# First norm of a two-layer backbone kernel: who computes the modulation, and in which order

## The chip, the cores and the metric

The kernel runs on one core of one Trainium2 chip. The metric is the device time of one execution in microseconds. Engines are called PE (TensorE), DVE (VectorE), ACT (ScalarE), POOL (GpSimd) and SP (the queue that issues most loads).

## The reference, cut to what matters

Two layers over 512 latent and 256 context tokens of width 1024. All modulation comes from two conditioning vectors (one for latents, one for context) through a SiLU and a large matrix, 9 x 1024 outputs a layer:

```python
sc = jax.nn.silu(c); scc = jax.nn.silu(c_ctx)
m  = (sc  @ w_mod[i] + b_mod[i]).reshape(Bsz, 1, N_MOD, D_MODEL)
mc = (scc @ w_mod[i] + b_mod[i]).reshape(1, 1, N_MOD, D_MODEL)
x  = _half_ffn(x,  norm_g[i, 0], m,  0, w1, w3, w2)   # then a mixer, then a second half FFN
xc = _half_ffn(xc, norm_g[i, 0], mc, 0, w1, w3, w2)
```

A half FFN norms its input (RMS over the width), multiplies by one plus a scale and adds a shift, both from the modulation, computes `silu(h @ w1) * (h @ w3) @ w2`, and adds half of that times a gate, also from the modulation. Nothing of the first half FFN can start before the first norm, and the norm's output needs scale (1024 values, eight tiles of 128) and shift (eight more) for both vectors. The gate (eight tiles) is needed only by the down-projection.

## The kernel before, in words

Activations lie transposed: `x` is 128 partitions x 8 chunks x 768 tokens. Each f32 product is made of three fp32r products, of a high and a low part of both operands: ACT writes the high part (`split_hi`, L1362, and `weight_hi`), DVE the low one (`split_lo`, L2014, and `weight_lo`), PE multiplies hi by hi, hi by lo and lo by hi (`gemm_step`, L698 to L702). Weights come in tiles of 128 x 1024 (512 KB) through two buffers `raw`, loaded by SP in a fixed order.

**The first norm.** The first 24 tiles of the modulation matrix are loaded whole: tiles 0 to 7 are the shift, 8 to 15 the scale, 16 to 23 the gate (`gmini`). A tile is either multiplied on PE (`PE_MINI`, L1325: eight f32 matmuls of two columns, the two vectors in `sc`; each shows in the trace as two instructions) or, in another layout, on DVE (`DVE_MINI`): one `dot` (L2019) per vector, a product of 128 x 1024 with the broadcast vector, with a sum along the row into `M`. Before the change seven tiles are PE's and nine DVE's, in order of number. ACT squares the eight chunks of `x`, POOL adds seven of them (`add_squares`, L2899), PE sums over the partitions with a matrix of ones (`norm_sums`, L751 and L754, its place is ahead of tile 11), ACT makes `rstd` by Ln and Exp (L1504, L1505). DVE does its eighteen dots, two weight splits among them, adds the bias, makes the scale `modA` (`prep`), and then runs `norm`: `scaled(j)` writes x times scale times rstd (L2292), ACT adds the shift (L1516, `xh`), `rest(j)` writes the low part (L2284, `xl`) and releases chunk j to PE. Four chunks are scaled before the first `rest`. PE then multiplies the first two weight tiles together (`gemm_pair`), chunk by chunk as they are released.

**The first FFN** (f = 0) has 22 hidden chunks in groups of 4, 6, 6, 6. A group multiplies its up tiles (two per hidden chunk), and then its eight down tiles (j = 0 to 7) into `x`. Group 0 is plain (`plain_pair`). Groups 1 to 3 use seven half-size products per chunk (`seven_products`, weights A11, S1, S2, S34, A12, A22), whose sums of weight blocks POOL prepares in DRAM by accumulating DMAs (`weight_sums`), starting right after its `add_squares`. Between all this DVE computes the remaining modulation. `gate_dots(i)`, i = 0 to 3, four dots each, stood ahead of and behind the hidden chunks 0 and 1. The later "mods" (120 tiles, two dots each) are placed by a table, `mod_places`: so many at an up chunk or down tile; their loads go through two buffers `mraw`, issued on ACT's queue two mods ahead (`next_mods`), each after the dots of the mod before last in the same buffer. `take_scb` applies the SiLU to the broadcast vectors (`scb`) that all those dots use; before the change that was ahead of the FFN.

Engines take their instructions in program order; waits are on semaphores.

Of the kernel before, what the change touches and what calls it, by code (L numbers as in the profile page):

```python
# [22 lines left out]
P = 128  # L23
# [128 lines left out]
def mod_places():  # L152
    where = []
    for f in range(3):
# [8 lines left out]
        if f == 0:  # L163
            place["down", 1, 2] = place["down", 2, 2] = 2
# [43 lines left out]
def build(nc, dr):  # L208
    ctx = ExitStack()
    with ctx:  # L210
# [70 lines left out]
        mini = [at(f"mini{j}", [P, D], XH + j * D) for j in range(2 * KC)]  # L281
        gmini = [at("gmini0", [P, 4, D], H + 4 * D), at("gmini1", [P, 4, D], H)]
# [129 lines left out]
        def sem(name):  # L412
# [3 lines left out]
        par_landed, con_landed, x_landed, out_stored = sem("par_landed"), sem("con_landed"), sem("x_landed"), sem("out_stored")  # L416
# [14 lines left out]
        sc_ready, eps_set, prep_done = sem("sc_ready"), sem("eps_set"), sem("prep_done")  # L431
# [19 lines left out]
        wdt_landed, wdt_hi, wdt_lo, dt_mm, dt_copied, dt_abs, dt_act, dt_set, dve_chain = (  # L451
            sem(n) for n in ("wdt_landed", "wdt_hi", "wdt_lo", "dt_mm", "dt_copied", "dt_abs", "dt_act", "dt_set", "dve_chain"))
# [49 lines left out]
        def heads(col, n, width):  # L502

            return col.unsqueeze(2).to_broadcast([P, n, width])

# [58 lines left out]
        def _(sp):  # L564
# [73 lines left out]
            for j in range(2 * KC):  # L638
                src = dr["wmk"][PE_MINI.index(j)] if j in PE_MINI else dr["wmn"][j]
                sp.dma_start(mini[j][:], src).then_inc(mini_landed[group(j)], 16)  # L640
                if j == KC:
                    sp.dma_start(con[:], dr["con"]).then_inc(con_landed, 16)
                if j in (10, 12):
                    s = j // 2 - 5
# [703 lines left out]
        def _(act):  # L1348
# [625 lines left out]
            for j in range(KC):  # L1974
                square(j, 0, x[:, j, :], T)
# [1133 lines left out]
```

## Time and profile before

| | us |
|---|---|
| median of 3 runs | 2787.57 (2786.97 to 2790.0) |
| the profiled execution, its own time | 2784.83 |
| span of the profile | 2783.1 |
| PE busy | 2675.1 (96%) |
| DVE busy | 2056.2 (74%) |
| ACT busy | 1176.3 (42%) |
| POOL busy | 390.2 (14%) |

Times in rows are microseconds from the start of the span. A row of the timeline gives the start, the length, engine, line, operation, output and inputs, the count merged into it, and in brackets how long the engine was idle before it and what ended that. A start with "q" behind the engine's name is that engine's queue issuing a DMA.

### The profile page before, as it was taken

How to read it: one execution, taken by the hardware profiler on the slowest of the kernel's cores; microseconds unless marked ns; L12 is line 12 of the kernel's file. 1: busy time of each engine (PE TensorE's matmuls, PEld its weight loads, DVE VectorE, ACT ScalarE, POOL GpSimd, SP SyncE). 2: the span in 40 equal slices, each digit the busy share in tenths (PEclk: the TensorE clock that was granted, in tenths of full speed). 3: DMA queues.
4: the chain of work that ended last, by engine and by line, in shares of the span. 5: the costliest groups of instructions: out<-in, count | busy, mean ns of one | idle time of the engine just before them, and what ended most of it. 6: DMA issues, size and time to landing. Idle time of an engine off the chain costs nothing.

```text
span 2783.1 us, 40131 instructions
## 1 busy us (share of the span) xinstructions
PE 2675.1 (96%) x15624; PEld 2512.6 (90%) x15624; DVE 2056.2 (74%) x3184; ACT 1176.3 (42%) x1860; POOL 390.2 (14%) x312
## 2 busy tenths in 40 slices
PE   5999999999988999999999999999999989999999
PEld 5999999998976899999999999999997775788898
DVE  7887878774558587878777877787878667666674
ACT  3233333346447644332323523242436866533342
POOL 3111111110012521111111211100022410211000
PEclk8999999999999999999999999999999999999999
DMA  9888989621120047889897589874522110378453
GB/s 347 209 228 248 274 252 267 169 67 54 59 62 1 1 143 203 245 224 281 229 274 212 137 221 258 248 214 131 165 69 83 61 46 1 114 201 235 145 165 125
DMA packets 161691, 464.13 MB, mean 167 GB/s; under 512 B 13281, under 2 KB 14433, under 8 KB 160609
## 3 DMA queue, kind: packets, MB, share of 16 engines
q1 hardware_dynamic: 87200, 247.65, 26.3%
q0 software_dynamic: 56448, 146.81, 24.3%
q10 hardware_dynamic: 17856, 67.12, 6.8%
q8 instruction: 125, 2.05, 0.3%
q14 instruction: 62, 0.50, 0.0%
HBM read 459.43 MB, written 148.90 MB: 219 GB/s over the span
## 4 chain that ended last, share of the span: by engine, by line
PE 78%; DVE 11%; DMA 5%; ACT 3%; issue 3%; POOL 0%; ACTq 0%; SPq 0%; DVEq 0%; POOLq 0%
PE banks L698 11%; PE banks L702 11%; PE banks L700 11%; PE banks L786 9%; PE banks L788 9%; PE banks L787 9%; DMA raw<-sums 4%; PE banks L705 3%; PE banks L709 3%; PE banks L707 3%; DVE banks L2019 1%; DVE tmp L2292 1%; PE banks L1233 1%; DVE wl L2086 1%; DVE wl L2014 1%
## 5 line engine op out<-in xcount | busy, mean ns | idle before, releaser
L1362 ACT ACTIVATE wh<-raw 128x1024 fp32r<-128x1024 f32 (+2 forms) x194 | 181.8, 937 | 611.8 <-PE banks L702 458.7
L2019 DVE SCALAR_TENSOR_TENSOR banks<-mraw,scb 128x1024 f32<-128x1024 f32 x240 | 304.9, 1270 | 11.6 <-DMA mraw<-in_wmn 7.9
L2014 DVE TENSOR_TENSOR wl<-raw,wh 128x1024 fp32r<-128x1024 f32 (+2 forms) x216 | 234.3, 1085 | 95.5 <-ACT wh L1362 93.2
L1427 ACT ACTIVATE wh<-raw 128x512 fp32r<-128x512 f32 (+1 forms) x210 | 161.6, 774 | 326.6 <-DMA raw<-sums 156.7
L698 PE MATMUL banks<-hh,wh 128*128 128x384 f32 x1056 | 270.4, 337 | 9.3 <-DVE wl L2014 9.0
L786 PE MATMUL banks<-xh,wh 128*128 128x384 f32 (+1 forms) x796 | 258.0, 324 | 12.8 <-DVE wl L2086 12.7
L702 PE MATMUL banks<-hh,wl 128*128 128x384 f32 x1056 | 269.9, 336 | 0.0
L700 PE MATMUL banks<-hl,wh 128*128 128x384 f32 x1056 | 269.7, 336 | 0.0
L788 PE MATMUL banks<-xh,wl 128*128 128x384 f32 (+1 forms) x796 | 256.6, 322 | 0.0
L787 PE MATMUL banks<-xl,wh 128*128 128x384 f32 (+1 forms) x796 | 256.5, 322 | 0.0
L698 PE MATMUL banks<-xh,wh 128*128 128x384 f32 x880 | 230.7, 343 | 21.4 <-DVE xl L2284 12.0
L700 PE MATMUL banks<-xl,wh 128*128 128x384 f32 x880 | 225.2, 336 | 0.0
L702 PE MATMUL banks<-xh,wl 128*128 128x384 f32 x880 | 224.9, 336 | 0.0
L2086 DVE TENSOR_TENSOR wl<-raw,wh 128x512 fp32r<-128x512 f32 (+1 forms) x210 | 180.9, 866 | 43.6 <-ACT wh L1427 43.5
L698 PEld LDWEIGHTS banks<-hh,wh 128*128 128x128 f32 x1056 | 191.5, 189 | 11.5 <-DVE wl L2014 11.2
L702 PEld LDWEIGHTS banks<-hh,wl 128*128 128x128 f32 x1056 | 192.3, 189 | 0.0
L700 PEld LDWEIGHTS banks<-hl,wh 128*128 128x128 f32 x1056 | 192.2, 189 | 0.0
L698 PEld LDWEIGHTS banks<-xh,wh 128*128 128x128 f32 x880 | 158.4, 189 | 29.9 <-issue 16.0
L786 PE MATMUL banks<-th,wh 128*128 128x384 f32 (+1 forms) x560 | 180.5, 322 | 0.0
L787 PE MATMUL banks<-tl,wh 128*128 128x384 f32 (+1 forms) x560 | 180.5, 322 | 0.0
L788 PE MATMUL banks<-th,wl 128*128 128x384 f32 (+1 forms) x560 | 180.5, 322 | 0.0
L786 PEld LDWEIGHTS banks<-xh,wh 128*128 128x128 f32 x796 | 150.0, 188 | 16.3 <-DVE wl L2086 16.3
(427 smaller groups left out, 6225.5 us busy)
## 6 DMA issues: line engine op xcount, KB each, us to landing
raw<-sums SPq DMA_DIRECT2D x140, 512.0 KB, 6.0
sums<-in_w POOLq DMA_DIRECT2D x88, 768.0 KB, 8.5
mraw<-in_wmn ACTq DMA_DIRECT2D x120, 512.0 KB, 5.7
a<-in_w SPq DMA_DIRECT2D x70, 512.0 KB, 4.3
sums<-in_w POOLq DMA_DIRECT2D x22, 1536.0 KB, 8.8
sums<-sums POOLq DMA_DIRECT2D x44, 768.0 KB, 9.6
raw<-in_w SPq DMA_DIRECT2D x80, 384.0 KB, 4.3
raw<-in_w SPq DMA_DIRECT2D x52, 512.0 KB, 3.9
```

The source lines that it names most:

```text
L698: pe.matmul(bank(h), W, tokens(rh, h), start=(k == 0), stop=False)
L700: pe.matmul(bank(h), W, tokens(rl, h), start=False, stop=False)
L702: mm = pe.matmul(bank(h), L, tokens(rh, h), start=False, stop=(k == nk - 1))
L705: pe.matmul(G[slot][:, a:b], W, rh[:, k, a:b], start=(k == 0), stop=False)
L786: pe.matmul(thirds(bank), W, rh(k), start=(k == 0), stop=False)
L787: pe.matmul(thirds(bank), W, rl(k), start=False, stop=False)
L788: mm = pe.matmul(thirds(bank), L, rh(k), start=False, stop=(k == 3))
L1362: act.activation(wh[slot][:, 0:nk * P], raw[slot][:, 0:nk * P], ACT.Copy).then_inc(hi_done, 1)
L1427: act.activation(W_HI[slot_of(name, last)], W_SRC[name], ACT.Copy).then_inc(w_hi, 1)
L2014: dve.tensor_tensor(wl[slot][:, 0:nk * P], raw[slot][:, 0:nk * P], wh[slot][:, 0:nk * P].bitcast(F32), ALU.subtract).then_inc(lo_done, 1)
L2019: return dve.scalar_tensor_tensor(B67[:], tile, 1.0, scv[:, s, :], ALU.mult, ALU.mult, accum_out=out)
L2086: dve.tensor_tensor(W_LO[to], W_SRC[name], W_HI[to].bitcast(F32), ALU.subtract).then_inc(w_lo, 1)
```

## The change

It deals the sixteen first tiles anew: PE gets 8 to 12, 0 to 2 and 4 to 6 in this order, DVE 13, 14, 15, 3 and, behind the scaling of the first chunks, 7. The loads follow that order, in eight groups; `x` is loaded in halves, the first weight tiles come ahead of them. Tiles 0 to 7 now lie where the gate tiles go later, so these are loaded after the shifts have been used. PE multiplies parameters by parameters into the norm's bank, a result nobody reads, eight times ahead of tile 8 and four times ahead of tiles 10 and 0 (512 columns, f32). The norm's sums move ahead of tile 0 and are one product, as DVE now adds all eight squares, which ACT writes to eight places of their own. Tiles 4 to 6 wait until ACT has made `rstd`, whose bank they use. The shift is added in two halves inside `norm`. The gate dots use `scb0` and stand one place later each; `take_scb` follows hidden chunk 1. Hidden chunk 2 has no mods of its own any more; down tile 5 of groups 1 and 2 has two instead of one.

```diff
-PE_MINI = (1, 3, 5, 7, 9, 11, 13)
-DVE_MINI = (0, 2, 4, 6, 8, 10, 12, 14, 15)
-MINI_GROUPS = ((0, 1, 2), (3, 4, 5, 6), (7, 8, 9, 10), (11, 12, 13), (14, 15))
+PE_MINI = (8, 9, 10, 11, 12, 0, 1, 2, 4, 5, 6)
+DVE_MINI = (13, 14, 15, 3, 7)
+MINI_GROUPS = ((8, 9, 13), (10, 11, 14), (12, 15), (0, 3), (1, 2), (4, 7), (5,), (6,))
+WARM = {8: 8, 10: 4, 0: 4}
...
         if f == 0:
-            place["down", 1, 2] = place["down", 2, 2] = 2
+            place["up", 2] = 0
+            place["down", 1, 2] = place["down", 2, 2] = place["down", 1, 5] = place["down", 2, 5] = 2
...
+                        if (f, g, i) == (0, 0, 1):
+                            load_gate_minis()
...
+            def load_gate_minis():
+                for q in range(2):
+                    sp.wait_ge(mini_mm, 2 + q)
+                    sp.wait_ge(mini_dot, (9, 12)[q])
+                    sp.dma_start(gmini[q][:], dr["wmn"][16 + 4 * q:20 + 4 * q].rearrange("t p n -> p t n")).then_inc(gmini_landed, 16)
+                sp.dma_start(wdt[:], dr["wdt"]).then_inc(gmini_landed, 16)
+
             sp.dma_start(par[:], dr["par"]).then_inc(par_landed, 16)
+            for s in range(2):
+                sp.dma_start(raw[s][:, 0:D], dr["w13"][s]).then_inc(raw_landed[s], 16)
             sp.dma_start(scb0[:], dr["ccb"]).then_inc(scb_landed, 16)
-            sp.dma_start(x[:], dr["x"]).then_inc(x_landed, 16)
...
+            for q, js in enumerate(MINI_GROUPS):
+                for j in js:
+                    src = dr["wmk"][PE_MINI.index(j)] if j in PE_MINI else dr["wmn"][j]
+                    sp.dma_start(mini[j][:], src).then_inc(mini_landed[q], 16)
+                if q < 2:
+                    half_k = slice(4 * q, 4 * q + 4)
+                    sp.dma_start(x[:, half_k, :], dr["x"][:, half_k, :]).then_inc(x_landed[q], 16)
+                if q == 0:
+                    sp.dma_start(con[:], dr["con"]).then_inc(x_landed[0], 16)
...
+                if n == 0:
+                    for a, b, _s in segs:
+                        mm = pe.matmul(NP[:, a:b], cst("ones"), ssq[:, a:b], start=True, stop=True)
+                    mm.then_inc(norm_sum, 1)
+                    return
...
             for j in PE_MINI:
-                if j == 11:
-                    pe.wait_ge(con_landed, 16)
+                for _ in range(WARM.get(j, 0)):
+                    pe.matmul(NP[:, 0:512], par[:, 0:P], par[:, 0:512], start=True, stop=True)
+                if j == 0:
+                    pe.wait_ge(x_landed[0], 32)
                     norm_sums(0, SEGS)
-
+                if j == 4:
+                    pe.wait_ge(rstd_ready, 1)
...
                 for j in range(KC):
+                    if n == 0 and j % 4 == 0:
+                        act.wait_ge(mini_dot, (9, 12)[j // 4])
...
-                        if 0 < f < 3 and ch == 1:
-                            take_scb(f + 2, scb)
+                        if f < 3 and ch == 1:
+                            take_scb(f + 2 if f else 1, scb)
...
+            act.wait_ge(par_landed, 16)
+            act.activation(sc[:].rearrange("p k s -> p (k s)"), pr("cc"), ACT.Silu).then_inc(sc_ready, 1)
+            split_hi(0, 0, 0, KC)
+            split_hi(1, 1, 0, KC)
             act.wait_ge(scb_landed, 16)
             act.activation(scb0[:], scb0[:], ACT.Silu).then_inc(scb_ready, 1)
...
             for j in range(KC):
-                square(j, 0, x[:, j, :], T)
...
+                if j % 4 == 0:
+                    act.wait_ge(x_landed[j // 4], (32, 16)[j // 4])
+                act.activation(squares[j][:], x[:, j, :], ACT.Square).then_inc(sq_done, 1)
             norm(0, SEGS, lambda j: None)
             load_scb(scb)
-            take_scb(1, scb)
...
                         def ahead():
+                            if f == 0 and 1 <= ch < 3:
+                                gate_dots(2 * ch - 1)
+                            if f < 3:
+                                dot_mods(f, ("up", ch))
+
+                        def behind():
                             if f == 0 and ch < 2:
                                 gate_dots(2 * ch)
...
+            def shift_batch(q):
+                dve.wait_ge(mini_mm, 2 + q)
+                dve.wait_ge(mini_dot, (8, 11)[q])
+                first_bias(4 * q, 3, 4).then_inc(mini_dot, 1)
+                dve.wait_ge(mini_dot, (9, 12)[q])
+
+            def first_between(q):
+                if q == 0:
+                    shift_batch(0)
+                    first_dots(7, 9)
+                if q == 1:
+                    shift_batch(1)
+
+            chain(dve.memset(eps[:], EPS))
+            split_lo(0, 0, KC)
+            split_lo(1, 1, KC)
+            dve.wait_ge(scb_ready, 1)
+            first_dots(13, 0)
+            for j in range(1, 4):
+                add_square(j)
+            first_dots(14, 2)
+            for j in range(4, KC):
+                add_square(j)
+            first_dots(15, 4)
+            first_dots(3, 6)
             dve.wait_ge(par_landed, 16)
             dve.wait_ge(mini_mm, 1)
...
             prep(0)
-            norm(0, SEGS, lambda s: None)
+            norm(0, SEGS, first_between)
...
-            add_squares(0, T)
+            pool.wait_ge(mini_landed[len(MINI_GROUPS) - 1], 16 * len(MINI_GROUPS[-1]))
             for g in (1, 2, 3):
                 weight_sums(0, g)
```

`first_dots(j, n)` is two dots of tile j, `add_square(j)` one add of 128 x 768 into `ssq`, `first_bias` two small adds.

## Rows read from the trace of the kernel before

**Rows 1.** The page: busy us, share of the span, instructions
```profile
PE 2675.1 (96%) x15624; PEld 2512.6 (90%) x15624; DVE 2056.2 (74%) x3184; ACT 1176.3 (42%) x1860; POOL 390.2 (14%) x312
```

**Rows 2.** Timeline of PE, 17 to 60 us
```profile
22.41 13.81 PE L1325 MATMUL banks<-sc,mini 128*128 128x2 f32 x64 [1.36 <-DMA mini<-in_wmn]
36.09 2.91 PE L751 MATMUL banks<-ssq,con 128*128 128x512 f32 x4
...
41.35 3.79 PE L1325 MATMUL banks<-sc,mini 128*128 128x2 f32 x32
57.09 0.98 PE L698 MATMUL banks<-xh,wh 128*128 128x384 f32 x2 [11.96 <-DVE xl L2284]
```

**Rows 3.** Windows: busy per engine; then PE's granted clock, DMA share, GB/s
```profile
45.00:46.00 1.00, 0.13 (x2) 0.04 (x1) 0.97 (x3) 0.98 (x2) 0.46 (x1) 0.54 0.48 193
...
61.00:62.00 1.00, 1.00 (x4) 1.00 (x4) 1.00 (x3) 0.78 (x2) 0.00 (x0) 0.50 1.06 264
62.00:63.00 1.00, 1.00 (x7) 1.00 (x7) 1.00 (x3) 0.34 (x1) 0.00 (x0) 0.93 1.12 284
```

**Rows 4.** Timeline of DVE up to the first norm's chunks
```profile
18.81 2.65 DVE L2019 SCALAR_TENSOR_TENSOR banks<-mini,scb 128x1024 f32<-128x1024 f32 x1
...
49.32 1.23 DVE L2019 SCALAR_TENSOR_TENSOR banks<-mini,scb 128x1024 f32<-128x1024 f32 x1
...
51.57 4.32 DVE L2292 SCALAR_TENSOR_TENSOR tmp<-x,modA,rstd 128x512 f32<-128x512 f32 x8
...
55.80 2.21 DVE L2284 SCALAR_TENSOR_TENSOR xl<-tmp,M,xh 128x512 fp32r<-128x512 f32 x4
```

**Rows 5.** Timeline of ACT: landings of x and weights, rstd
```profile
13.71 1.58 ACT L1479 ACTIVATE sq<-x 128x768 f32<-128x768 f32 x2 [5.45 <-DMA x<-in_x]
...
33.40 1.06 ACT L1362 ACTIVATE wh<-raw 128x1024 fp32r<-128x1024 f32 x1 [2.68 <-DMA raw<-in_w]
...
41.64 1.28 ACT L1504 ACT_TABLE_LOAD   x1 [7.19 <-PE banks L754]
...
45.15 0.84 ACT L1505 ACTIVATE rstd<-sq 128x768 f32<-128x768 f32 x1
```

**Rows 6.** Timeline around the end of the first pair of products
```profile
67.66 1.28 ACT L1375 ACT_TABLE_LOAD   x1
...
76.33 0.79 ACT L1391 ACTIVATE tmp<-banks 128x768 f32<-128x768 f32 x1
...
77.73 0.61 PE L698 MATMUL banks<-xh,wh 128*128 128x384 f32 x2 [1.42 <-DVE wl L2014]
```

**Rows 7.** Timeline of DVE at the end of group 0's up tiles
```profile
127.98 0.95 DVE L2049 TENSOR_TENSOR tmp<-tmp,banks 128x768 f32<-128x768 f32 x1
```

**Rows 8.** Timeline of ACT's DMA queue, down tiles of groups 1 and 2
```profile
293.67 0.33 ACTq L1368 DMA_DIRECT2D mraw<-in_wmn  x1
...
432.01 0.33 ACTq L1368 DMA_DIRECT2D mraw<-in_wmn  x1
```

**Rows 9.** Timeline of DVE at the turn to the next group
```profile
304.36 0.88 DVE L2203 SCALAR_TENSOR_TENSOR x<-banks,modG,x 128x256 f32<-128x256 f32 x2 [0.64 <-PE banks L702]
...
312.85 0.69 DVE L2086 TENSOR_TENSOR wl<-a,wh 128x512 fp32r<-128x512 f32 x1
...
444.41 0.88 DVE L2203 SCALAR_TENSOR_TENSOR x<-banks,modG,x 128x256 f32<-128x256 f32 x2 [0.64 <-PE banks L702]
```

**Rows 10.** Timeline of PE: the A12 product of group 2's first chunk
```profile
314.60 0.33 PE L786 MATMUL banks<-xh,wh 128*128 128x384 f32 x1
```

**Rows 11.** Landing of mod tiles: whole run (page, last number), 285 to 310, 425 to 450
```profile
mraw<-in_wmn ACTq DMA_DIRECT2D x120, 512.0 KB, 5.7
...
DMA to landing us min/median/max: 4.1/6.1/8.2
...
DMA to landing us min/median/max: 5.0/7.0/9.0
```

**Rows 12.** Timeline of POOL at the second norm
```profile
540.58 1.40 POOL L2896 COPY ssq<-sq 128x768 f32<-128x768 f32 x1 [15.87 <-ACT sq L1479]
```

More of the change, by code:

```diff
@@ L277, in pr @@
             return par[:, PCOL[n][0]:PCOL[n][1]]
-        mini = [at(f"mini{j}", [P, D], XH + j * D) for j in range(2 * KC)]
-        gmini = [at("gmini0", [P, 4, D], H + 4 * D), at("gmini1", [P, 4, D], H)]
+        mini = [at(f"mini{j}", [P, D], (H if j < KC else XH - KC * D) + j * D) for j in range(2 * KC)]
+        gmini = [at(f"gmini{q}", [P, 4, D], H + 4 * q * D) for q in range(2)]
+        squares = [ssq, sq[0], sq[1], tmp[0], tmp[1], tmp[2], tmp[3], rstd]
         scb0 = at("scb0", [P, 2, D], HID + 2 * HC * T - 3 * T)
@@ L504, in heads, with mini_out @@
             return col.unsqueeze(2).to_broadcast([P, n, width])
+        def mini_out(j, n=1):
+            bank = G[0][:, 0:512] if j >= KC else G[0][:, 512:1024] if j < 4 else NP
+            return bank[:, 2 * j:2 * (j + n)]
         def group(j):
@@ L1615, in ab_in_act @@
                     if c == 3:
-                        act.wait_ge(wdt_landed, 16)
-                        act.activation(wdh[:], wdt[:], ACT.Copy).then_inc(wdt_hi, 1)
+                        act.wait_ge(gmini_landed, 48)
+                        act.activation(wdh[:], wdt[:], ACT.Copy).then_inc(dt_act, 1)
                         act.activation(ea[:, 0, :], pr("alog"), ACT.Exp).then_inc(dt_act, 1)
@@ L2268, in gate_dots @@
                         dve.wait_ge(mini_dot, n0 + 2 * q + s)
-                        dot(gmini[q // 4][:, q % 4, :], s, scb, M[:, 16 + q, s:s + 1]).then_inc(mini_dot, 1)
+                        dot(gmini[q // 4][:, q % 4, :], s, scb0, M[:, 16 + q, s:s + 1]).then_inc(mini_dot, 1)
                 dve.wait_ge(mini_dot, n0 + 4 * i + 4)
@@ L2857, in _, with add_square, first_bias @@
                     dot(mini[j][:], s, scb0, M[:, j, s:s + 1]).then_inc(mini_dot, 1)
-                if q in (6, 7):
-                    split_lo(q - 6, q - 6, KC)
+            def add_square(j):
+                dve.wait_ge(sq_done, j + 1)
+                if j > 1:
+                    dve.wait_ge(ssq_acc, j - 1)
+                dve.tensor_tensor(ssq[:], ssq[:], squares[j][:], ALU.add).then_inc(ssq_acc, 1)
+            def first_bias(j, n_pe, n):
+                bias = pr("bmod")[:, j:j + n].unsqueeze(2).to_broadcast([P, n, 2])
+                dve.tensor_tensor(M[:, j:j + n_pe, :], mini_out(j, n_pe).rearrange("p (t s) -> p t s", s=2), bias[:, 0:n_pe], ALU.add)
+                return dve.tensor_tensor(M[:, j + n_pe:j + n, :], M[:, j + n_pe:j + n, :], bias[:, n_pe:n], ALU.add)
@@ L2864, in _ @@
-            for js, src in ((slice(1, 14, 2), pairs), (slice(0, 15, 2), M), (slice(15, 16), M)):
-                n_ = len(range(16)[js])
-                chain(dve.tensor_tensor(M[:, js, :], src[:, js, :], pr("bmod")[:, js].unsqueeze(2).to_broadcast([P, n_, 2]),
-                                        ALU.add))
+            dve.wait_ge(mini_dot, 8)
+            chain(first_bias(KC, 5, KC))
             prep(0)
-            norm(0, SEGS, lambda s: None)
+            norm(0, SEGS, first_between)
```

62 lines of the change are left out of this document (18 added, 44 removed).

## The prediction

> **What bounds the kernel now.** I read the page first. PE is busy for 96% of the span [rows 1], so what the change touches, the first 57 us, is nearly the only long stretch without useful matmuls, and what it can give is small beside 2783 us.
>
> Then the timeline, engine by engine. PE works through seven narrow tiles (two columns each), squeezes the norm's sums in between, and then stands idle for 11.96 us until the first real matmul at 57.09, released by DVE's `xl` [rows 2]. DVE has eighteen dots to do, a dot is 2.65 us while POOL adds squares and 1.30 us after that, the last starts at 49.32, and only then, at 51.57, can it scale the first chunk, though `rstd` was there at 45.99 [rows 4, 5]. So DVE's dots set the start: 57.09 = 51.57, plus 4.23 for four scaled chunks, plus 1.1 for `rest(0)`.
>
> The clock needs care. The granted clock is 1.00 in the windows before 45 and half in 45.1 to 62.1 [rows 3], but durations tell of more: 64 narrow instructions take 13.81 us from 22.41, 32 take 3.79 us from 41.35 [rows 2]. One tile is 16 of them: 3.45 us before 41.4, 1.90 us after. I read this as 1.2 GHz up to about 41.5, 2.4 GHz up to 45.1, 1.2 GHz again until 62.1. It rose some 5.2 us after wide matmuls began (36.09 to 41.5, 57.09 to 62.1) and fell 3.6 us after they ended (41.4 to 45.1), although narrow tiles filled those 3.6 us. I use these two delays below.
>
> **Landings.** `x` lands at 13.71, the second weight tile at 33.40 [rows 5]; between them 13 tiles, the constants and two weight tiles land, 8072 KB in 19.69 us, 410 KB/us. The new order on the same queue gives: first group 12.5, half of `x` with constants 17.2, second group 20.9, other half 24.7, then 27.1, 29.6, 32.1, 34.6, 35.9, 37.1.
>
> **A. The start of the first up-projection.** DVE loses 8 of 18 dots ahead of the norm's scaling (five tiles are ten dots, two of them tile 7's, moved behind it) and gains seven adds; a 128x768 add is about 0.95 us. POOL no longer runs beside it, so a dot is 1.30. In order: tile 13 to 15.1, three adds behind ACT's squares to 21.7, tile 14 to 24.3, four adds to 29.2, tiles 15 and 3 to 34.4, bias and prep to about 35. It isn't late any more.
>
> PE is. `sc` is ready near 3.9. A 512-column f32 matmul is 5.26 us x 512/1536 = 1.75 us at 1.2 GHz [rows 2], so 0.88 at 2.4. Eight fillers: 5.2 us slow (3 of them), five fast, to 13.5. Tiles 8 and 9 at 1.90: 17.3; there the clock falls. Four fillers, 5.2 + 0.9: 23.4. Tiles 10 and 11: 27.2. Tile 12, slow: 30.7. Four fillers: 36.8. The two sums of 768 columns, now fast: 38.1. ACT then needs what it took from 41.56 to 45.99 [rows 5]: `rstd` at 42.5.
>
> Two paths lead from there to the first real matmul.
> - DVE: 4.25 (four scaled) + 0.5 (bias of the first shifts) + 2.65 (tile 7's two dots, which now stand ahead of `rest(0)`) + 1.2 = 51.1.
> - PE: tiles 0 to 2, 3.6 us fast and the rest slow, to 45.5; tiles 4 to 6, slow, 3 x 3.45 = 10.35, to 55.9. They must be through before the first matmul, as PE works in order.
>
> PE ends last: 55.9 for 57.09, a gain of 1.2 us. DVE's supply and ACT's, delayed by waits on the shifts, still run ahead of it, and the second shift bias waits only for tile 6. The pair of products that follows starts at half clock as before and keeps its 19.2 us. Bounds from the rows: if the third fillers and tiles 0 to 2 all run fast, 51.5 (gain 5.6); if the third fillers and the sums are slow and tiles 0 to 2 too, 60.9 + 0.1 (loss 3.9). I take the walk's value, whose delays are the measured ones.
>
> **B. The Silu table.** Today ACT loads Silu's table at 67.66, for `take_scb`, while it waits for nothing else, and the first Silu of `G[0]` starts at 76.33, straight behind the split of the third tile [rows 6]. With `take_scb` one chunk later, the table load of 1.28 us falls between that split and this Silu, which frees the bank that the third product needs. It would end at 77.12 + 1.28 = 78.4 on today's scale against 77.67, when `wl` was there [rows 6]: +0.8. Bounds 0 (the load is hoisted) and 1.3.
>
> **C. Costed at nothing.** Gate dots: ch 0 loses four, ch 2 exchanges four mod dots for four gate dots. PE has no wait from 77.73 to the end of this group, and the last multiply, at 127.98 [rows 7], follows PE's product by 0.2 us, so at most 0.2 comes back. If that cover went, four dots would be 5.3 us. On SP, `load_gate_minis` stands after tiles 2 and 3 and waits for the second shift batch, near 57; behind it only loads wait that need the split of tile 2 at 76. The gate tiles (4 MB, 10 us) then land by 70, needed near 80. On POOL, `weight_sums` starts at 37 for 31, but its first block is then free of the initial loads; at the next norm POOL had waited 15.87 us for ACT [rows 12], more than these 6 us and the earlier start together. Were that gone, ACT's squares would wait. DVE's split of the first weights comes earlier, in idle time.
>
> **D. The two mods that move to the sixth down tile of groups 1 and 2.** Each is 2.65 us more of DVE in one tile, and one more load in a chain of two buffers. In group 1 the second mod's load is the one issued at 293.67 [rows 8]. With the page's 5.7 us to landing [rows 11] it lands at 299.4. Then: two dots to 302.0, `x` of j=6 to 303.2, three splits of 0.6 to 305.0, the two dots of j=6 to 307.7. `x` of j=7 started at 304.36 [rows 9]: DVE is 3.3 us late. ACT, which issues loads behind dots, issues the next one at 308.1, it lands 0.45 after DVE wants it. From that `x` on DVE runs without a gap to the split for A12, which ends at 313.45 and is wanted by PE at 314.60 [rows 9, 10], slack 1.15. Stall: 3.3 + 0.45 - 1.15 = 2.6. In group 2 the load is that of 432.01, landing 437.7, dots to 440.4, and by the same steps `x` at 446.0 for 444.41: 1.6 + 0.45 - 1.15 = 0.9 (slack taken as equal). Together +3.5. Bounds by landings seen just there [rows 11]: at 4.1 and 5.0 us the stalls are 0.95 and 0.1, sum 1.0; at the stretches' medians of 6.1 and 7.0 some 3.4 and 3.6, sum 7.0; at the maxima near 11. I take the page's median, as only few of the neighbours' issues are these. PE being in order, what is lost isn't given back.
>
> **Sum:** -1.2 + 0.8 + 0 + 3.5 = +3.1 us; less 0.2 at most from C: +2.9. Against the profiled execution, 2784.8, that is 2787.7. The median of the runs, 2787.6, lies 2.7 above the profiled one, so I give 2790.5.
>
> **Rivals.** A difference under 0.2% (5.6 us) can't be told from no change here.
> 1. *The moved dots are hidden* (D = 0: landings as short as 4 us, or slack that I don't see). -1.2 + 0.8 - 0.2 = -0.6: 2787.0. For it: f=0 had two such tiles without a PE wait. Against: those lie four tiles ahead of the turn to the next group, these two.
> 2. *The clock stays up through the narrow tiles*, as they follow wide ones without a gap. Walk: fillers to 13.5, tiles 17.3, fillers 20.8, tiles 24.7, tile 12 29.0, fillers 32.5, sums 33.8, `rstd` 38.2, tiles 0 to 2 39.5, 4 to 6 45.2, DVE's path 46.9. The first real matmul at 47, and the pair all fast: its 19.2 us hold 5.0 at half clock, so 16.7. It ends at 63.7 for 76.3, -12.6. Sum -12.6 + 0.8 - 0.2 + 3.5 = -8.5: 2779.1. Against: the fall at 45.1, with narrow tiles running to 45.14 [rows 2, 3]. The Trainium skill (TensorE: Matmul & The Clock Gate, Why this matters for your kernels) asks for no idle gaps between bursts to keep the full clock; by that rule narrow tiles back to back would hold it and the sum would be this rival's, but this trace does not agree, by the fall just named.
> 3. *DVE falls further behind* (the other side): landings as in the stretches, D = 7.0: +6.4, 2794.0. It decides once a mod takes more than about 6.5 us to land at both turns; for it speak the medians of 6.1 and 7.0 [rows 11].
> 4. *The fillers don't raise the clock*, the change doesn't do what it says: all at 1.2 GHz PE ends tile 12 at 42.1, the sums at 51.7, tile 6 at 72.4: +15.3 + 4.1 = +19.4, 2807. Against: two rises behind wide matmuls.
>
> **Chances.** Likeliest 0.52 (its own range 2787 to 2794), rival 1 0.20, rival 2 0.10, rival 3 0.15, rival 4 0.03. Faster by over 0.2%: rival 2 and a tail, 0.12. Slower: rival 4, most of rival 3, a tail of the likeliest, 0.22. Within: 0.66. The range 2783 to 2797 leaves out rivals 2 and 4 and tails.
>
> **What would show it.** In the profile after: the first matmul of the pair at 55.9, released by PE's own narrow tiles, not by `xl`; narrow tiles 4 to 6 at 0.21 us an instruction; `rstd` near 42.5, dots of 1.23 us throughout; an ACT table load right ahead of the first Silu of `G[0]`; new PE waits on `wl` at the first A12 of groups 2 and 3 of the first FFN. The prediction is wrong if PE is on 2.4 GHz in tiles 4 to 6, if the sums come much before 38, if the waits at the turns are missing or above 8 us, or if POOL's sums come late.

## The result and the profile after

The changed kernel is slower by a quarter of a per cent: 2794.56 us in the median of 18 runs (2785.86 to 2803.76), the kernel before 2789.84 in 18 runs beside them (2775.01 to 2797.72), ratio 1.0027 with a 95% interval of 1.0015 to 1.0039. The ratio is worth 7.5 us, the medians differ by 4.7. Single executions of one kernel lie up to 23 us apart (the two ends for the kernel before), so each profile below is one draw from such a spread: the profiled execution of the changed kernel took 2803.39 us, at the upper end of its own runs.

I read the start first. Timeline of PE in the kernel after, up to the first real matmul, to be held against [rows 2]:

```profile
3.92 8.52 PE L1339 MATMUL banks<-par 128*128 128x512 f32 x16 [3.92 <-ACT sc L1994]
13.24 3.73 PE L1347 MATMUL banks<-sc,mini 128*128 128x2 f32 x32 [0.81 <-DMA mini<-in_wmn]
16.84 5.38 PE L1339 MATMUL banks<-par 128*128 128x512 f32 x8
22.05 3.63 PE L1347 MATMUL banks<-sc,mini 128*128 128x2 f32 x32
29.63 3.58 PE L1347 MATMUL banks<-sc,mini 128*128 128x2 f32 x16 [3.95 <-DMA mini<-in_wmn]
33.07 5.86 PE L1339 MATMUL banks<-par 128*128 128x512 f32 x8
38.76 1.45 PE L766 MATMUL banks<-ssq,con 128*128 128x512 f32 x4
40.05 16.61 PE L1347 MATMUL banks<-sc,mini 128*128 128x2 f32 x96
56.52 0.99 PE L712 MATMUL banks<-xh,wh 128*128 128x384 f32 x2
```

The idle 11.96 us of [rows 2] are gone and PE's own narrow tiles stand right ahead of the first real matmul. It comes at 56.52, only 0.57 us sooner. DVE was ready well before, as its timeline shows: it waits for `rstd` and scales from 43.42 on, where it began at 51.57 [rows 4]. PE's row shows the other half: tiles 0 to 2 and 4 to 6, 96 instructions, run until the first real matmul.

```profile
43.42 4.32 DVE L2314 SCALAR_TENSOR_TENSOR tmp<-x,modA,rstd 128x512 f32<-128x512 f32 x8 [7.00 <-ACT rstd L1527]
```

Then the end of the first pair of products, which answers to [rows 6]: ACT's timeline, PE's first matmul of the third product, and windows of one microsecond behind it (busy time by engine, then PE's granted clock, DMA share, GB/s).

```profile
74.69 1.06 ACT L1384 ACTIVATE wh<-raw 128x1024 fp32r<-128x1024 f32 x1 [10.84 <-PE banks L716]
75.77 1.28 ACT L1413 ACT_TABLE_LOAD   x1
77.06 0.81 ACT L1413 ACTIVATE tmp<-banks 128x768 f32<-128x768 f32 x1
```

```profile
78.02 0.63 PE L712 MATMUL banks<-xh,wh 128*128 128x384 f32 x2 [2.38 <-ACT tmp L1413]
```

```profile
78.00:79.00 1.00, 0.98 (x4) 1.00 (x5) 1.00 (x2) 0.86 (x2) 0.00 (x0) 0.71 1.17 215
79.00:80.00 1.00, 1.00 (x4) 1.00 (x4) 1.00 (x2) 0.81 (x1) 0.00 (x0) 0.50 1.07 274
80.00:81.00 1.00, 1.00 (x4) 1.00 (x4) 1.00 (x3) 0.00 (x0) 0.25 (x1) 0.50 1.11 397
81.00:82.00 1.00, 1.00 (x5) 1.00 (x5) 1.00 (x1) 0.00 (x0) 0.98 (x1) 0.58 0.92 299
```

The table load stands between the split and the first Silu of `G[0]`, and PE waits 2.38 us where it waited 1.42. The wait brought more than itself: behind it the clock falls to half for some 3.4 us, which costs another 1.7 us of work (1 minus the clock, summed over the four windows). Behind the wait of 1.42 in the kernel before it didn't fall.

Now the turns to the next group. The profile's waits of PE, 300 to 350 and then 430 to 480 us (total, times, longest):

```profile
PE banks L805 <- DVE wl L2109: 2.3, 1, 2.3
PE banks L805 <- DVE wal L2109: 1.5, 1, 1.5
...
PE banks L805 <- DVE wl L2109: 6.6, 2, 5.6
```

The kernel before has 0.9 us of such waits in the first stretch and none in the second. DVE's timeline at both turns, against [rows 9] (the reads of the accumulator behind each dot are left out):

```profile
302.27 1.23 DVE L2042 SCALAR_TENSOR_TENSOR banks<-mraw,scb 128x1024 f32<-128x1024 f32 x1 [1.47 <-DMA mraw<-in_wmn]
...
310.20 0.87 DVE L2226 SCALAR_TENSOR_TENSOR x<-banks,modG,x 128x256 f32<-128x256 f32 x2
...
319.27 0.68 DVE L2109 TENSOR_TENSOR wl<-a,wh 128x512 fp32r<-128x512 f32 x1
...
453.55 0.87 DVE L2226 SCALAR_TENSOR_TENSOR x<-banks,modG,x 128x256 f32<-128x256 f32 x2
...
458.31 1.23 DVE L2042 SCALAR_TENSOR_TENSOR banks<-mraw,scb 128x1024 f32<-128x1024 f32 x1
...
463.06 1.23 DVE L2042 SCALAR_TENSOR_TENSOR banks<-mraw,scb 128x1024 f32<-128x1024 f32 x1 [3.46 <-DMA mraw<-in_wmn]
...
465.88 0.68 DVE L2109 TENSOR_TENSOR wl<-a,wh 128x512 fp32r<-128x512 f32 x1
```

And why the dot at 463.06 had to wait: ACT and its DMA queue at the second turn.

```profile
447.53 1.15 ACT L1449 ACTIVATE wh<-raw 128x512 fp32r<-128x512 f32 x2 [8.72 <-DVE banks L2042]
...
454.16 1.06 ACT L1449 ACTIVATE wh<-raw 128x1024 fp32r<-128x1024 f32 x1 [5.47 <-DVE banks L2042]
...
459.63 0.34 ACTq L1390 DMA_DIRECT2D mraw<-in_wmn  x1
460.07 0.63 ACT L1449 ACTIVATE wh<-a 128x512 fp32r<-128x512 f32 x1 [2.92 <-DVE banks L2042]
```

The issue at 459.63 stands right behind the dot that ends at 459.5, which frees the buffer; its mod reaches DVE 3.4 us later, and the three splits that the A12 product needs stand behind that dot in DVE's order. The splits of ACT wait for DVE too (8.72, 5.47 and 2.92 us "<-DVE banks"), since ACT issues each load only when the dots before it are done, and its weight splits stand behind that. In the kernel before, ACT waited 4.87, 5.09 and 0.92 us ahead of the same splits, and PE ended those waits. So a late DVE makes the loads late, and ACT's part of the splits. What came back to DVE by the mod was 3.46 us; by ACT's splits it was 0.44 us at either turn (DVE's idle time ahead of the `wl` split at 311.90 and 455.25). PE stands still for 5.59 us and then runs at half clock, as the windows show:

```profile
466.62 0.69 PE L805 MATMUL banks<-xh,wh 128*128 128x384 f32 x1 [5.59 <-DVE wl L2109]
```

```profile
320.00:330.00 10.00, 9.99 (x48) 9.99 (x49) 8.29 (x12) 4.33 (x7) 1.22 (x1) 0.83 0.88 262
...
466.00:470.00 4.00, 3.38 (x11) 3.38 (x12) 3.74 (x6) 0.52 (x1) 0.00 (x0) 0.50 1.08 215
470.00:475.00 5.00, 5.00 (x28) 5.00 (x27) 3.14 (x5) 2.93 (x5) 0.77 (x1) 0.90 0.88 290
```

**Where the time went.** I compared the start of the same ScalarE instruction in two timelines: its lag behind the kernel before. Each figure below is the median of the lags within 12 us of that time, one profiled execution of each kernel (the experiments are told in the next section).

| us in the kernel before | 100 | 165 | 270 | 400 | 560 | 1120 | 2770 |
|---|---|---|---|---|---|---|---|
| after | +1.8 | +1.1 | +0.5 | +5.0 | +14.4 | +14.4 | +18.6 |
| after_old_mods | +0.9 | +3.6 | +3.3 | +1.0 | +2.1 | +2.2 | +8.4 |
| after_early_silu | -1.6 | -1.6 | -0.9 | +0.9 | +8.0 | +8.8 | +6.3 |
| after_both_undone | -1.5 | +1.2 | +0.9 | +1.3 | +2.6 | +3.7 | +4.0 |
| before_new_mods | +3.8 | +3.6 | +3.7 | +10.4 | +14.0 | +13.6 | +12.5 |
| before_dots_only | +0.5 | -0.4 | +0.5 | +0.4 | +1.4 | -0.8 | -5.8 |
| dots_only_again | +3.7 | +3.4 | +3.1 | +6.8 | +10.9 | +10.2 | +15.1 |
| before_one_mod_moved | +3.1 | +2.3 | +3.7 | +8.1 | +9.3 | +9.0 | +10.1 |
| mods_at_down0 | -1.7 | -1.7 | -1.8 | -2.9 | +5.3 | +3.1 | +0.7 |
| three_more_on_dve | -1.3 | +1.5 | +1.1 | +0.9 | +0.9 | +0.6 | +6.3 |
| no_fillers | -1.2 | +1.6 | +1.2 | +0.4 | +0.3 | -0.8 | +2.2 |
| gate_dots_behind | -1.5 | -1.4 | -1.9 | -4.4 | -3.4 | -3.7 | -8.2 |
| start_and_table | -7.0 | -7.0 | -5.8 | -6.5 | -4.1 | -3.1 | +2.4 |

The first line is the answer for the one execution: next to nothing until 270, 4.5 us at the first turn, 9.4 at the second, the rest late in the run, where the change touches nothing and where the other lines swing by 5 to 6 us either way.

A caution on the first columns. Four of these kernels (the two of before_dots_only, before_new_mods and before_one_mod_moved) have the code of the kernel before up to 100 us, and yet three of them are 3.1 to 3.8 us behind it there. PE's wait ahead of the third product, 1.42 us in the profile of the kernel before, is 2.53 to 3.39 us in all four. The Silu of `scb`, which stands ahead of ACT's split of that tile, waits longer for its transfer. In the kernel before it starts at 71.80, after a wait of 2.86 us; in before_new_mods, for one:

```profile
74.87 1.91 ACT L1376 ACTIVATE scb<-scb 128x2048 f32<-128x2048 f32 x1 [5.93 <-DMA scb<-in_ccb]
79.04 1.01 PE L699 MATMUL banks<-xh,wh 128*128 128x384 f32 x2 [3.39 <-DVE wl L2015]
```

So the profile of the kernel before is a lucky one at this place, and a lag of up to 4 us between two single profiles need not come from an edit. For the turns, read how a line grows from 270 to 560: +13.9 for the change, +10.3 for before_new_mods, +7.8 for dots_only_again, +5.6 for before_one_mod_moved, and -1.5 to +1.7 in the six kernels whose mods are at their old places with no dots added.

### The profile page after: what moved, and what is told of

Its sections match the earlier page's. It is cut to its first block, busy times and chain, and to the rows that moved or that the text cites. A ratio compares the mean times of both kernels' runs of the same rounds, so it can differ in the third digit from the quotient of the medians.

```text
span 2801.6 us, 40306 instructions
## 1 busy us (share of the span) xinstructions
PE 2708.0 (97%) x15716; PEld 2534.7 (90%) x15716; DVE 2044.1 (73%) x3178; ACT 1175.5 (42%) x1860; POOL 374.2 (13%) x305
## 4 chain that ended last, share of the span: by engine, by line
PE 80%; DVE 10%; DMA 4%; ACT 3%; issue 2%; POOL 0%; SPq 0%; ACTq 0%; DVEq 0%; POOLq 0%
PE banks L805 11%; PE banks L807 11%; PE banks L806 11%; PE banks L712 10%; PE banks L714 10%; PE banks L716 10%; PE banks L719 3%; PE banks L723 3%; PE banks L721 3%; DMA mraw<-in_wmn 2%; DMA raw<-sums 1%; PE banks L1252 1%; DVE tmp L2314 1%; PE banks L1091 1%; DVE wl L2037 1%
## 5 line engine op out<-in xcount | busy, mean ns | idle before, releaser
L712 PEld LDWEIGHTS banks<-hh,wh 128*128 128x128 f32 x1056 | 191.4, 189 | 12.5 <-DVE wl L2037 12.2
```

The costliest lines, as they stand in the source:

```text
L712: pe.matmul(bank(h), W, tokens(rh, h), start=(k == 0), stop=False)
```

## The experiments

Medians stand beside those of the kernel before on the same chip: 2787.91 (34 runs) for the first four; 2786.06 (34) for before_dots_only, mods_at_down0, three_more_on_dve and no_fillers; 2786.19 (31) for dots_only_again, before_one_mod_moved, gate_dots_behind and start_and_table.

**after_old_mods.** The changed kernel with all mods at their old places:

```diff
-            place["up", 2] = 0
-            place["down", 1, 2] = place["down", 2, 2] = place["down", 1, 5] = place["down", 2, 5] = 2
+            place["down", 1, 2] = place["down", 2, 2] = 2
```

> The changed kernel with the mods back in their old places (two at hidden chunk 2, one at down tile 5 of groups 1 and 2). Theory M (the two moved mods cost most of the loss, through DVE's lateness at the turns to groups 2 and 3): no PE wait on weights above 1 us at either turn, and a time of the kernel before, -4 to +3 us; hidden chunk 2 then has eight dots, which may cost up to 3 us on PE in group 0. Theory S (the loss lies ahead of the first FFN's group 1, in the late Silu table load and the clock that falls behind it): turns clean too, but the time stays 4 us or more above before.

2786.90 us, ratio 0.9998 (0.9983 to 1.0012): the loss is gone, and with it the waits at both turns. PE still waits 2.38 us for the table load.

**after_early_silu.** The moved mods kept, `take_scb(1, scb)` back ahead of `ffn(0)`:

```diff
-                        if f < 3 and ch == 1:
-                            take_scb(f + 2 if f else 1, scb)
+                        if 0 < f < 3 and ch == 1:
+                            take_scb(f + 2, scb)
...
             load_scb(scb)
+            take_scb(1, scb)
             ffn(0, KC, 1, T, T)
```

> The changed kernel with take_scb back ahead of the first FFN, nothing else. Theory S: PE's wait for the third weight tile is 1.4 us instead of 2.4, the granted clock stays 1.00 behind it, together 2.5 us less than the changed kernel, and with it most of the loss gone. Theory M: 1 to 2.5 us less than the changed kernel, which leaves 4 us or more above before, and PE still waits 3 to 7 us in sum at each of the turns to groups 2 and 3.

2793.88 us, ratio 1.0021 (1.0004 to 1.0037). In the profile the wait is 1.42 again, without the fall of the clock, and the lag at 100 us is 3.4 us better, 1.0 of it because the first real matmul came at 55.48 for 56.52. In the median that can't be told from nothing. PE still waits 3.5 and 4.0 us on weight splits at the two turns.

**after_both_undone.** Both of these diffs together; what stays is the first norm and the gate dots.

> The changed kernel with both undone: old places of the mods and early take_scb. Both theories: only the new start is left, whose first real matmul stood 0.6 us earlier than before, so -3 to +2 us against before. If it is slower by 4 us or more, something else in the start costs, such as the later weight sums on POOL.

2786.00 us, ratio 0.9990 (0.9974 to 1.0006). It differs from after_early_silu by the mods alone, and is 7.9 us faster by the medians. The lag is -1.5 us at 100 and +1.2 at 165. Between the two stands a wait that neither the kernel before nor the change has (waits of PE, 120 to 145 us):

```profile
PE banks L711 <- DVE hl L2078: 3.4, 1, 3.4
```

Eight dots, four for the gate and four for mods, stand there ahead of the product of up chunk 2. The wait stands in after_old_mods, no_fillers and three_more_on_dve too, at 3.40 or 3.41 us: every kernel with the gate dots of the change and the mods left in chunk 2. This is followed up in gate_dots_behind.

**before_new_mods.** The kernel before with the new places alone (the first diff, the other way).

> The kernel before with the new places of the mods alone: none at hidden chunk 2, two at down tile 5 of groups 1 and 2. Theory M: PE waits of 2 to 7 us in sum at each of the two turns that the kernel before does not have, and 5 to 13 us slower than before. Rival (the stalls at the turns come only together with the new start, by its later weight sums and other phase of the loads): within 2 us of before, and clean turns.

2799.21 us, ratio 1.0041 (1.0022 to 1.0060). The places alone cost as much as the whole change or more. PE at the turns:

```profile
317.14 0.66 PE L787 MATMUL banks<-th,wh 128*128 128x384 f32 x1 [2.84 <-DVE wl L2087]
325.81 0.44 PE L787 MATMUL banks<-xh,wh 128*128 128x384 f32 x1 [2.91 <-DVE wl L2087]
468.53 0.45 PE L787 MATMUL banks<-xh,wh 128*128 128x384 f32 x1 [3.29 <-DVE wl L2087]
```

So the cause was placed. Open was what of a moved mod costs: its load in the chain of two buffers, or its 2.65 us of DVE.

**before_dots_only.** The kernel before; at down tile 5 of groups 1 and 2 the two dots of the mod already there are done twice, with no load more:

```diff
                 for m in MODS[f][2].get(key, ()):
+                    if f == 0 and key in (("down", 1, 5), ("down", 2, 5)):
+                        dve.wait_ge(mod_landed[m % 2], 16 * (m // 2) + 16)
+                        dve.wait_ge(mod_dot, 2 * m)
+                        for q in range(2):
+                            chain(dot(mraw[m % 2][:], q, scb, M[:, 24 + m, q:q + 1]))
                     dot_mod(m, scb, 1 if f == 0 else f + 2, mraw)
```

> The kernel before, its mods in their old places, with two more dots on the tile already there at down tile 5 of groups 1 and 2 (same values written twice): the 2.65 us of DVE that the moved mods bring, without their load. Theory L (the load is what costs: the second mod waits for a tile that is issued behind the dots of the one before, and lands 5 to 8 us later): waits of PE at the turns 0 to 1.5 us each, 0 to +4 us against before. Rival W (DVE's plain work costs): most of the +11 us that the new places alone cost, at least +7.

2795.21 us, ratio 1.0040 (1.0024 to 1.0055). My theory that an added load was the cost fell: dots without one cost about as much. (The added dots also hold the buffer longer, so the next load is issued later; this run doesn't part that delay from DVE's own time.) But the profiled execution, 2779.08 us, was the fastest of twelve, and showed almost none of it (+1.4 at 560). A profile that disagrees with its own median explains nothing, so I ran the same kernel again.

**dots_only_again.** No edit.

> The kernel before with the two extra pairs of dots at down tile 5 of groups 1 and 2, as in before_dots_only, to see a second profiled execution: there the profile showed a lag of only 1.4 us at 600 us while the median was 9 us above the kernel before. Theory W (VectorE has no room for 2.65 us more at these turns, and how much of it shows depends on how late the transfers are in the one execution): the median again 6 to 11 us above the kernel before, and this profile shows new PE waits on wl of 2 to 8 us in all at 300 to 350 and 430 to 480 us. Rival: the median of the first measurement was a chance of it; then 0 to 3 us above, and no waits at the turns.

2793.99 us, ratio 1.0015 (0.9995 to 1.0035), profiled at 2799.96. Together the two measurements lie 8 to 9 us up by medians, 4 to 11 by ratios, and the interval of the second reaches just below 1. This profile shows what the other didn't:

```profile
321.77 0.44 PE L786 MATMUL banks<-xh,wh 128*128 128x384 f32 x1 [2.95 <-DVE wl L2091]
464.84 0.44 PE L786 MATMUL banks<-xh,wh 128*128 128x384 f32 x1 [2.29 <-DVE wl L2091]
```

Its DVE had two waits just ahead of the four dots that the fast execution had not, one for ACT's split and one for the mod; the split had itself waited 7.91 us for its weight tile:

```profile
297.51 0.85 ACT L1362 ACTIVATE wh<-raw 128x768 fp32r<-128x768 f32 x1 [7.91 <-DMA raw<-in_w]
...
298.39 0.96 DVE L2014 TENSOR_TENSOR wl<-raw,wh 128x768 fp32r<-128x768 f32 x1 [0.91 <-ACT wh L1362]
300.04 1.23 DVE L2019 SCALAR_TENSOR_TENSOR banks<-mraw,scb 128x1024 f32<-128x1024 f32 x1 [0.69 <-DMA mraw<-in_wmn]
```

In the fast one the same split and dot of DVE started at 293.53 and 294.48, with no wait ahead of either. My reading is that the extra work eats the slack in which DVE had absorbed transfers a microsecond or two late. Two profiles of this kernel fit it; they don't prove it.

**before_one_mod_moved.** The kernel before with one mod moved, from up chunk 2 to down tile 5 of group 1:

```diff
-            place["down", 1, 2] = place["down", 2, 2] = 2
+            place["up", 2] = 1
+            place["down", 1, 2] = place["down", 2, 2] = place["down", 1, 5] = 2
```

> The kernel before with one mod only moved, from up place 2 to down tile 5 of group 1; the second stays. Theory M with costs that add: the wait at the turn of group 1 (300 to 350 us) is the 3 to 6 us of the runs with both, the turn of group 2 clean, and the median 4 to 7 us above the kernel before. Rival: the two moves amplify each other (one alone hides in slack, the second doesn't): under 2 us for one alone.

2792.81 us, ratio 1.0015 (0.9996 to 1.0034), 6.6 us up by medians. The first turn costs 5.6 us of waits, the second is clean but for 0.8 us. The waits are those of one turn alone, and the median is up by about half of what both cost; the time by itself isn't told from none, as the interval reaches below 1.

**mods_at_down0.** The changed kernel with the early `take_scb`, and the two mods at down tile 0 in place of 5, as far from the turn as can be:

```diff
-            ... = place["down", 1, 5] = place["down", 2, 5] = 2
+            ... = place["down", 1, 0] = place["down", 2, 0] = 2
```

> The changed kernel with early take_scb and the two mods at down tile 0 instead of 5 of groups 1 and 2, five tiles further from the turn. If nearness to the turn decides, the waits at the turns are those of the old places (0 to 2 us in sum) and the time is that of the kernel with both undone (0.999 of before) or up to 2 us better, as hidden chunk 2 is rid of its eight dots. If the chain of loads through two buffers is saturated over the whole row of down tiles, lateness is carried to the turn all the same: 3 us or more worse than with both undone.

2792.11 us, ratio 1.0020 (1.0006 to 1.0034), against 1.0021 with tile 5. In the profile the turns have 1.0 us of waits, but there is a new one of 4.5 us on `wl`, at 427.24, near the first down tiles of group 2, and the lag grows by 8.2 us from 400 to 560. In group 1 nothing of the kind is seen in this execution. The cost moves with the dots; it isn't a property of the turn.

**three_more_on_dve.** After_both_undone, with tiles 6 and 5 also on DVE, their dots and tile 7's in the gap in which DVE waits for `rstd`:

```diff
-PE_MINI = (8, 9, 10, 11, 12, 0, 1, 2, 4, 5, 6)
-DVE_MINI = (13, 14, 15, 3, 7)
+PE_MINI = (8, 9, 10, 11, 12, 0, 1, 2, 4)
+DVE_MINI = (13, 14, 15, 3, 7, 6, 5)
...
             prep(0)
+            first_dots(7, 8)
+            first_dots(6, 10)
+            first_dots(5, 12)
             norm(0, SEGS, first_between)
```

> Both undone, and the narrow tiles 5 and 6 given to DVE, whose dots with those of tile 7 now fill the 7 us in which DVE waited for rstd. Theory (PE's narrow tiles at half clock set the start): the first real matmul at 50 to 51.5 instead of 56.5, the gain of 5 to 6 us goes through to the end, -6 to -9 us against before. Rival (DVE's path sets it after all): first real matmul not before 54.

2787.29 us, ratio 1.0011 (0.9998 to 1.0023): nothing of the expected gain. The first real matmul did come 5 us sooner, at 52.06, but the third product didn't:

```profile
52.06 0.98 PE L711 MATMUL banks<-xh,wh 128*128 128x384 f32 x2 [3.01 <-DVE xl L2306]
...
74.93 0.84 PE L711 MATMUL banks<-xh,wh 128*128 128x384 f32 x2 [3.21 <-DVE wl L2037]
```

```profile
70.76 1.91 ACT L1396 ACTIVATE scb<-scb 128x2048 f32<-128x2048 f32 x1 [5.35 <-DMA scb<-in_ccb]
72.58 1.04 ACT L1383 ACTIVATE wh<-raw 128x1024 fp32r<-128x1024 f32 x1
```

ACT's split of the third weight tile stands behind the Silu of `scb`, and that waits for its transfer until 70.76. PE waits 3.21 us and then works at half clock (0.84 us for a pair of matmuls instead of 0.51). A second limit lay close behind the first.

**no_fillers.** After_both_undone with `WARM = {}`.

> Both undone, and no filler matmuls: parameters are never multiplied, the rest is the same. Theory: the sums run at half clock but start some 5.8 us earlier, tiles 0 to 2 slow, and the first real matmul comes within 1 us of that with fillers (56.5); the time is the same within 2 us. If the fillers earn what they cost, it comes 3 us or more later.

2785.64 us, ratio 1.0006 (0.9992 to 1.0019). The first real matmul comes at 55.71, with fillers at 55.34.

```profile
32.67 2.91 PE L765 MATMUL banks<-ssq,con 128*128 128x512 f32 x4
35.37 20.48 PE L1346 MATMUL banks<-sc,mini 128*128 128x2 f32 x96
```

Without them the sums start 5 us sooner and run at half clock, as do all narrow tiles. The fillers do raise the clock, but cost as much time as they save.

**gate_dots_behind.** After_both_undone with no gate dots left for chunk 2:

```diff
                         def ahead():
-                            if f == 0 and 1 <= ch < 3:
-                                gate_dots(2 * ch - 1)
+                            if f == 0 and ch == 1:
+                                gate_dots(2)
...
                         def behind():
-                            if f == 0 and ch < 2:
-                                gate_dots(2 * ch)
+                            if f == 0 and ch == 0:
+                                gate_dots(0)
+                                gate_dots(1)
+                            if f == 0 and ch == 1:
+                                gate_dots(3)
```

> after_both_undone, whose profile shows a new PE wait of 3.4 us on hl at 120 to 145 us, with the gate dots put so that none is left for up place 2: two batches behind place 0, one ahead of and one behind place 1. Theory G (eight dots ahead of the product of place 2, four for the gate and four for mods, are what is late there; moving the mods away, as the change does, is what pays for moving the gate dots): the wait of 3.4 us on hl goes, the lag behind the kernel before at 165 us is -1.5 to 0 where it was +1.2, and the median is 1 to 3 us under the kernel before, which can't be told from none. Rival: the wait comes from something else of the first norm (the order of loads), and stays.

2781.96 us, ratio 0.9985 (0.9967 to 1.0004). The wait on `hl` is gone and the lag at 165 us is -1.4 for +1.2; the time leans to faster and isn't told from none. So the later gate dots are what fills chunk 2, and moving two mods out of it is what makes room for them.

**start_and_table.** All that was learnt: three_more_on_dve and gate_dots_behind, `take_scb` late as in the change, and Silu's table loaded early by a Silu of one column, which waits for no transfer:

```diff
             load_scb(scb)
-            take_scb(1, scb)
+            act.activation(few[:, 6:7], eps[:, 0:1], ACT.Silu)
             ffn(0, KC, 1, T, T)
```

> three_more_on_dve with three things more: the gate dots as in gate_dots_behind, take_scb late as in the change, and Silu's table loaded early by a Silu of one column at the old place of take_scb. In three_more_on_dve the first real matmul came at 52.06, 5 us before that of the kernel before, but PE waited 3.21 us for the third tile, and ScalarE's split of it stood behind a Silu of scb that waited for its transfer until 70.8. Theory T (that transfer is what swallowed the gain): the third pair begins at 71.5 to 73.5 us for 74.93, after a wait of 1.4 to 2 us, no half clock behind it, the lag at 100 us is -4 to -5 and at 165 us -3 to -5, the median 3 to 5 us under the kernel before. Rival: the landing of the third weight tile itself sets 74.9, and the lag at 100 us stays at -1 to -2.

2780.78 us, ratio 0.9968 (0.9951 to 0.9985): the only version that beats the kernel before. PE's and ACT's timelines:

```profile
51.06 0.98 PE L711 MATMUL banks<-xh,wh 128*128 128x384 f32 x2 [2.42 <-DVE xl L2306]
...
70.72 0.62 PE L711 MATMUL banks<-xh,wh 128*128 128x384 f32 x2 [1.42 <-DVE wl L2037]
```

```profile
63.15 1.28 ACT L2004 ACT_TABLE_LOAD   x1
64.44 0.20 ACT L2004 ACTIVATE few<-eps 128x1 f32<-128x1 f32 x1
68.34 1.06 ACT L1383 ACTIVATE wh<-raw 128x1024 fp32r<-128x1024 f32 x1 [3.70 <-PE banks L715]
```

The third product starts at 70.72, 4.2 us ahead of three_more_on_dve and 7.0 ahead of the kernel before, and the clock stays up. That is 2 to 3 us more than I expected; some of it is that the clock was up 3.0 us after the first real matmul, for 5.0 in the kernel before (57.09 to 62.1), as the windows show:

```profile
53.00:54.00 1.00, 1.00 (x5) 1.00 (x4) 1.00 (x3) 0.00 (x0) 0.00 (x0) 0.51 1.04 352
54.00:55.00 1.00, 1.00 (x7) 1.00 (x7) 1.00 (x3) 0.00 (x0) 0.00 (x0) 1.00 1.01 385
```

The lag of -7.0 us at 165 has shrunk to -3 at 1120 through new waits on `wl` in the first FFN, 1.3, 1.1 and 1.6 us among them, so the start isn't handed on whole either. The profiled execution, 2787.26 us, was the slowest of the ten. Three edits were made at once: the rows above tie the gain at 70 us to the two on ACT, but how the 5.4 us by the medians divide between these and the gate dots (4.2 us in gate_dots_behind, with an interval that overlaps) isn't shown.

## Why the prediction was wrong, step by step

It forecast no measurable change, 2790.5 with a range of 2783 to 2797. The median, 2794.56, lies in the range, but the ratio shows a loss, which had 0.22. The difference was forecast at +2.9 us; the medians give 4.7, the ratio 7.5. The runs beside it gave the kernel before 2789.84, for the 2787.57 on which I built, so that the median falls into the range, and next to rival 3's 2794.0, is partly chance.

- **A, the start: right.** PE ends last, at 56.52 for 55.9; `rstd` was ready at 43.3 for 42.5; DVE and ACT ran ahead. The walk missed a wait of 3.95 us for tile 12, which landed at 29.63 for 27.1 while PE was there 1.5 us sooner than walked. Fillers 2.0 us and tiles 0 to 2 and 4 to 6 1.2 us shorter than walked made up for most of it. In five other profiles with this start the first real matmul came at 55.25 to 55.56. The clock rose and fell much as read from [rows 2, 3]: in both kernels it fell with narrow tiles running, here 4.1 us after the sums. Rival 2 and rival 4 fell, though raising the clock bought nothing: without fillers the first real matmul comes within 0.4 us (no_fillers).
- **B, the table load: mechanism right, size low.** The wait grew by 0.96 us for 0.8. I had not counted that a wait of 2.38 us would be followed by half clock: 1.7 us more in this execution. The whole is worth 2.4 us by the lags at 100 us (3.4 less the 1.0 of an earlier start) and nothing that the medians could show. The base was a single profile, too: in the four others with the old code up to there PE waited 2.53 to 3.39 us and the third product began at 78.22 to 79.29, later than in the changed kernel (78.02). Against those the late `take_scb` loses nothing.
- **C, costed at nothing: right as a sum, wrong as parts.** The later gate dots, with the mods left in chunk 2, cost some 2.8 us (after_both_undone against after_early_silu, +1.2 and -1.6 at 165 us), and taking two mods out of chunk 2 gives them back. POOL was never late: at the next norm it waits 26.56 us for ACT, where it waited 15.87 [rows 12].
- **D, the moved mods: the step that failed, by its size.** Place and mechanism were as told: DVE late at `x` of j=7, a load issued late behind dots, a PE wait on the A12 split at both turns. The sizes were not. Group 1: `x` of j=7 is at 310.20 for 304.36; less the lag of 0.5 that is 5.3 us late, where I had 3.3. The reason stands in the row at 302.27: the moved dots themselves waited 1.47 us for their mod, and the tile before them had come late too. PE waits 3.8 us and then runs at 0.83 of the clock for 10 us (1.7 us); less the 0.9 us of waits that the kernel before has there this is 4.6, where the lag grows by 4.5 and I had 2.6. Group 2: `x` of j=7 is late by 453.55 - 444.41 - 5.0 = 4.1 us for 1.6, and the landing that DVE waits for costs 3.46 for 0.45. PE waits 6.6 us, and the clock behind it takes 2.2 more (half of 3.38 busy us to 470, a tenth of the 5 to 475): 8.8, where I had 0.9 and the lag grows by 9.4. D is thus near 14 us in this execution, 11.4 by the ratio of before_new_mods, and about 8 by that of the whole change against after_old_mods; predicted 3.5, with 11 as the far bound. Of the cases on record rival 3 is the nearest, DVE further behind; its price of 7.0 came from late landings alone.

Three things were wrong within D. I laid one dot pair more into a timetable that had just enough room and carried forward little more than the delay of that pair. The loads behind it came later in turn: 0.45 us for the next one in my sum, 1.47 us ahead of the moved dots at the first turn and 3.46 us at the second in the trace. ACT's weight splits, also behind those issues in ACT's order, added 0.44 us of waiting at each. I treated the landing as the unknown, where the dots alone cost 4 to 11 us with no load added. And I priced a PE wait at its own length, while in this execution the longest one at each turn, 2.33 and 5.59 us, was followed by a stretch at half clock. That isn't so every time, as the last section shows.

What stays open: how much of the late variation (the last column of the table) follows from the first FFN. The lines don't move together there, and no run separates it. Whether the delay of ACT's splits could be taken out by issuing the mods' loads from another queue wasn't tried.

## What to carry to other kernels

Where an engine off the bound is 87% busy (DVE had 34.6 of 40 us from 290 to 330), an extra 2.65 us isn't safely hidden by the average slack: here it cost 4 to 11 us over two turns in the medians and ratios, and next to nothing in one lucky execution. If one engine issues loads behind another's work and its own work stands behind those issues, follow the delay round that loop at least once. When a start is sped up, look for the next thing that arrives at a fixed time: here the 5 us reached the third product only when the wait for `scb` had been taken out of ACT's way. And when a profile and the median disagree, as in before_dots_only, take a second profile before telling a cause.

## What the runs showed of the hardware

- What follows a wait of PE isn't fixed by its length. These are all waits of PE over 1.3 us from 60 to 540 us in the fourteen profiles. Behind the seventeen of 1.3 to 1.8 us the granted clock stayed at 2.4 GHz each time. Of the thirty of 2.2 to 3.4 us, 22 were followed by half clock, often for 3 to 4 us, and eight weren't. The same wait of 2.88 us at the end of group 0 (139.22) is followed by half clock in the kernel before, and its twin of 2.87 us (141.02) in the changed kernel isn't, although 2.38 us were enough at 78.02. Behind 4.49 and 5.59 us the clock was at half. The Trainium skill (TensorE: Matmul & The Clock Gate, Why this matters for your kernels) asks for PE to be kept free of longer gaps in mid-kernel; the rows agree.
- A table load is 1.28 us and the Silu behind it starts at once, at 77.06 behind 75.77. The Trainium skill (ScalarE: Activation LUTs, What ACT_TABLE_LOAD costs) has the same 1.28 us and a drain beside it, 2.66 us in all; in this place the wait of PE grew by 0.96 only and the split ahead of the load ends at 75.75, so the drain isn't seen on either side.
- The same kernel on the same chip differed by up to 23 us from execution to execution (2779.08 to 2802.44 in before_dots_only). A transfer can differ with it: `scb`, issued at 66.3 to 66.8 us in five profiles with the same code up to there, let ACT's Silu start 5.3 to 8.4 us later.
